# Attention's value products with the values stationary on two column tiles, and ended groups' transposed sums turned back

## What is computed

```
s = jnp.einsum('bqkgd,bnkd->bkgqn', qc, k_cmp)
s = s.astype(jnp.float32) - slopes[:, :, None, None] * dist
p_cmp = masked_softmax(s, dist >= 0)
o_cmp = jnp.einsum('bkgqn,bnkd->bqkgd', p_cmp.astype(dt), v_cmp)
imp = jnp.einsum('bkgqn,nj->bkqj', p_cmp, ov)
...
o = gc[..., 0:1] * o_cmp + gc[..., 1:2] * o_slc + gc[..., 2:3] * o_win
```

## Time and profile before

| | us |
|---|---|
| median of 3 runs | 1056.08 |
| lowest and highest | 1053.9, 1059.67 |
| the profiled execution | 1058.48 |
| its span in the trace | 1056.7 |
| of it, attention (first scores to first SSD transposition) | 273.66 |

### The profile page before, as it was taken

One profiled execution on the slowest core, in us unless ns is written; L12 is line 12 of the kernel. 1 busy time (PEld: TensorE's weight loads), 2 busy tenths in 40 slices (PEclk: granted clock), 3 DMA queues, 4 the chain that ended last, 5 costly groups with the idle time before them and its releaser, 6 DMA issues.

```text
span 1056.7 us, 14288 instructions
## 1 busy us (share of the span) xinstructions
PE 1027.7 (97%) x4759; PEld 617.8 (58%) x4760; DVE 643.5 (61%) x1630; ACT 323.4 (31%) x766; POOL 175.4 (17%) x214
## 2 busy tenths in 40 slices
PE   8999999999999999999999999999989999999997
PEld 4544475444546877778779885555564444444443
DVE  3331121455454777776643898765578688877985
ACT  3321121111133766565665763332110000000000
POOL 0030051111000400000000400211021333323333
PEclk8999999999999999999999999999999999999999
DMA  7310042012000200000000504232649869999432
GB/s 262 103 45 28 1 82 79 1 40 84 20 1 1 81 2 1 1 2 2 1 1 1 200 2 133 100 120 80 238 161 367 294 234 345 338 383 340 137 113 91
DMA packets 73687, 119.23 MB, mean 113 GB/s; under 512 B 14016, under 2 KB 53152, under 8 KB 73632
## 3 DMA queue, kind: packets, MB, share of 16 engines
q1 hardware_dynamic: 62544, 87.55, 24.6%
q0 software_dynamic: 11088, 30.95, 8.3%
HBM read 105.37 MB, written 21.50 MB: 120 GB/s over the span
## 4 chain that ended last, share of the span: by engine, by line
PE 51%; DVE 12%; issue 3%; DMA 3%; ACT 2%; POOL 0%; POOLq 0%; DVEq 0%; ACTq 0%
PE ps L1804 14%; PE ps L1150 9%; PE ps L1814 7%; PE ps L2127 5%; PE ps L1118 4%; PE ps L1129 4%; PE ps L1171 3%; PE ps L2137 2%; DMA big_w<-hn_dram,misc 2%; DVE ring_gate_up L1276 1%; DVE big_w L1618 1%; PE ps L2158 1%; DVE big_u L2346 1%; ACT big_u L1226 1%; DVE misc L291 1%
## 5 line engine op out<-in xcount | busy, mean ns | idle before, releaser
L1618 DVE STREAM_TRANSPOSE big_w<-big_w 32x256 f32<-32x256 f32 x384 | 167.3, 436 | 34.7 <-DMA big_w<-hn_dram,misc 28.4
L1804 PE MATMUL ps<-ring_gate_up,big_w 128*128 (+1 forms) x400 | 179.9, 593 | 1.9 <-DVE big_w L1618 1.5
L517 PE MATMUL ps<-big_w,big_u 128*128 128x512 f32 (+1 forms) x448 | 175.8, 547 | 1.7 <-DMA big_w<-in_w_in 1.7
L517 PEld LDWEIGHTS ps<-big_w,big_u 128*128 128x128 f32 x448 | 84.2, 193 | 78.5 <-issue 71.9
L1804 PEld LDWEIGHTS ps<-ring_gate_up,big_w 128*128 128x128 f32 x400 | 73.9, 190 | 85.6 <-issue 85.6
L1150 PEld LDWEIGHTS ps<-ring_down,big_u 128*128 128x128 f32 x912 | 109.7, 192 | 15.7 <-issue 12.1
L1150 PE MATMUL ps<-ring_down,big_u 128*128 128x65 f32 x912 | 116.3, 273 | 0.5 <-DVE big_w L1303 0.4
L1226 ACT ACTIVATE big_u<-ps 128x512 f32<-128x512 f32 (+1 forms) x126 | 69.4, 582 | 112.9 <-PE ps L1129 112.7
L1276 DVE CUSTOM_DVE_ANT_0 ring_gate_up<-ps,ring_down 128x384 f32<-128x384 f32 (+7 forms) x128 | 73.8, 629 | 43.2 <-PE ps L1118 42.7
L1218 ACT ACTIVATE ring_gate_up<-ring_gate_up,big_w 128x64 f32<-128x64 f32 (+8 forms) x192 | 92.2, 555 | 1.1 <-DVE big_w L1276 1.1
L1814 PE MATMUL ps<-ring_down,big_w 128*128 x200 | 90.0, 593 | 0.6 <-ACT big_w L1848 0.6
(11 more groups left out here) (389 smaller groups left out, 1351.2 us busy)
## 6 DMA issues: line engine op xcount, KB each, us to landing
ring_gate_up<-in_w_gate SPq DMA_DIRECT2D x16, 1024.0 KB, 10.4
ring_gate_up<-in_w_up SPq DMA_DIRECT2D x16, 1024.0 KB, 13.2
ring_down<-in_w_down SPq DMA_DIRECT2D x16, 1024.0 KB, 14.8
misc<-in_x SPq DMA_DIRECT2D x16, 512.0 KB, 4.0
big_w<-in_w_in SPq DMA_DIRECT2D x6, 1024.0 KB, 7.2
big_w<-in_w_out SPq DMA_DIRECT2D x8, 512.0 KB, 5.2
hn_dram<-big_u SPq DMA_DIRECT2D x8, 512.0 KB, 2.6
out<-ring_gate_up SPq DMA_DIRECT2D x8, 512.0 KB, 3.8
```

The lines of the kernel that those rows point to most:

```text
L517: last = nc.tensor.matmul(ps[:, b, 0:width], uT[:, k, c * P:(c + 1) * P], wbuf[:, n % 2, k, 0:width], start=(k == 0), stop=(k == KD - 1))
L1618: last = nc.vector.transpose(dst[j * 32:(j + 1) * 32, :, i * 32:(i + 1) * 32], src[i * 32:(i + 1) * 32, :, j * 32:(j + 1) * 32])
L1804: last = nc.tensor.matmul(ps[:, 2 + b, :], xT[:, b, k, :], ring_gu[:, bass.ds(at + k * 2 * D_EXP, BANK)], start=(k == 0), stop=(k == KD - 1))
```

## The change

In WIN and SEL groups the two operands of the value product change places: 64 columns of values of group g are stationary, on column tile g of the array (output partitions 64g to 64g+63), and the transposed weights of all heads of the slot stream past them, 128, 256 or 512 columns. The blocks are transposed in another order for that (key block, group, head). The sums come out transposed, head dimension by query, in bank 6. When a group has ended, ACT copies them to SBUF (`copy_values`), PE turns them back with four transpositions (`turn_values`), and DVE reads the turned bank. CMP groups keep the weights stationary, now with both groups in one 128-row product against block-diagonal values (L1175 of the new kernel); their product with the overlap table is one of its own (L1170), into another bank, for chunks 4 to 7. The rows' sums of weights no longer come from a column of ones but from the exponentials themselves (`accum_out`). Banks 4, 5 and 7 serve transposed weights, turned sums, importance, selection and the SSD constants in turn. `values(j-2)` runs as a whole ahead of `transposes(j-1)`. WIN and SEL groups are read by DVE one iteration later.

```diff
-        return [(g, r, b) for i, g, r in heads_of(j) for b in range(len(key_blocks(br, c)))]
+        return [(g, r, b) for b in range(len(key_blocks(br, c))) for g in range(NG) for r in pairs]
...
+    turned = [gi for gi, (br, c) in enumerate(groups) if br != CMP]
+    turns_before = lambda gi: sum(1 for x in turned if x < gi)
+    turn_at = {last_slot[groups[gi]] + 3: gi for gi in turned}
+    imp_at = {last_slot[CMP, c] + 2: c for c in sel_count}
+    bank_users, copy_use, sel_use, imp_use, turn_use, prep_use = [], [], {}, {}, {}, None
+    for j in range(J + 3):
+        if j in imp_at:
+            imp_use[imp_at[j]] = len(bank_users)
+            bank_users.append((imp_read, sel_count[imp_at[j]]))
+        if j in turn_at:
...
+            turn_use[turn_at[j]] = len(bank_users)
+            bank_users.append((o_read, turn_at[j] + 1))
...
-            if use >= 2:
-                pe.wait_ge(*bank_users[use - 2])
-            return 4 + use % 2
+            if use >= 3:
+                pe.wait_ge(*bank_users[use - 3])
+            return bank_of(use)
...
-        def values(j, a, b):
+        def bank_is_free(gi):
+
+            if groups[gi - 1][0] == CMP:
+                pe.wait_ge(o_read, gi)
+            else:
+                pe.wait_ge(oT_copied, turns_before(gi))
+
+        def compressed_values(j):
 
             gi, br, c, pairs = slots[j]
-            if a == 0:
-                if j == first_slot[br, c] and gi >= 1:
-                    pe.wait_ge(o_read, gi)
-                pe.wait_ge(wT_done, copies_before[j + 1])
-            blocks = blocks_of(j)
-            w = HD + 17 if br == CMP else HD + 1
-            for x in range(a, b):
-                g, r, blk = blocks[x]
-                if br == CMP:
-                    for g in range(NG):
-                        rows = slice(g * 64, (g + 1) * 64)
-                        last = nc.tensor.matmul(ps[:, 6 + g, r * w:(r + 1) * w], weightsT(j, 0)[rows, x * P:(x + 1) * P],
-                                                v_cmp[rows, 0:w], start=True, stop=True)
-                    continue
-                at = key_blocks(br, c)
-                last = nc.tensor.matmul(ps[:, 6 + g, r * w:(r + 1) * w], weightsT(j, x // 4)[:, (x % 4) * P:(x % 4 + 1) * P],
-                                        vals[br][:, at[blk], g, :], start=(blk == 0), stop=(blk == len(at) - 1))
-            if b == len(blocks) and b > a:
-                last.then_inc(pv_done, 1)
+            pe.wait_ge(wT_done, copies_before[j + 1])
+            rows = [weightsT(j, 0)[:, r * P:(r + 1) * P] for r in pairs]
+            if c in sel_count:
+                bank = transpose_bank(imp_use[c])
+                for r in pairs:
+                    nc.tensor.matmul(ps[:, bank, r * NG * N_BLK:(r + 1) * NG * N_BLK], rows[r], v_cmp[:, NG * HD:CMP_V],
+                                     start=True, stop=True)
+            if gi >= 1:
+                bank_is_free(gi)
+            for r in pairs:
+                last = nc.tensor.matmul(ps[:, O_BANK, r * P:(r + 1) * P], rows[r], v_cmp[:, 0:NG * HD], start=True, stop=True)
+            last.then_inc(pv_done, 1)
+
+        def values(j):
+
+            gi, br, c, pairs = slots[j]
+            if j == first_slot[br, c]:
+                bank_is_free(gi)
+            pe.wait_ge(wT_done, copies_before[j + 1])
+            blocks, m = key_blocks(br, c), len(pairs)
+            for b, blk in enumerate(blocks):
+                for g in range(NG):
+                    x = (b * NG + g) * m
+                    last = nc.tensor.matmul(ps[g * HD:(g + 1) * HD, O_BANK, pairs[0] * P:(pairs[-1] + 1) * P],
+                                            vals[br][:, blk, g, 0:HD], weightsT(j, x // 4)[:, x % 4 * P:(x % 4 + m) * P],
+                                            start=(b == 0), stop=(b == len(blocks) - 1))
+            last.then_inc(pv_done, 1)
+
+        def turn_values(gi):
+
+            pe.wait_ge(oT_copied, turns_before(gi) + 1)
+            bank = transpose_bank(turn_use[gi])
+            for r in range(GQ):
+                last = nc.tensor.transpose(ps[:, bank, r * P:(r + 1) * P], o_T[:, turns_before(gi) % 2, r * P:(r + 1) * P],
+                                           ident[:, :])
+            last.then_inc(o_turned, 1)
...
+            if 2 <= j < J + 2 and slots[j - 2][1] != CMP:
+                values(j - 2)
+            if j in turn_at:
+                turn_values(turn_at[j])
...
-                    z_pieces(piece_at[j][1], piece_at[j][2])
                 transposes(j - 1, k)
-            if n_t == 0 and j in piece_at:
-                z_pieces(piece_at[j][1], piece_at[j][2])
-            if v < n_v:
-                values(j - 2, v, n_v)
...
-                last = nc.scalar.activation(w, w, ACT.Exp, bias=neg[:, br, h:h + 1], scale=-1.0)
+                last = nc.scalar.activation(w, w, ACT.Exp, bias=neg[:, br, h:h + 1], scale=-1.0,
+                                            accum_out=den[c % 2][:, br, h:h + 1])
...
+        def copy_values(gi):
+            act.wait_ge(pv_done, last_slot[groups[gi]] + 1)
+            nc.scalar.activation(o_T[:, turns_before(gi) % 2, :], ps[:, O_BANK, :], ACT.Copy).then_inc(oT_copied, 1)
...
         for j in range(J + 1):
+            if j in turn_at:
+                copy_values(turn_at[j])
...
+            bank = O_BANK if br == CMP else bank_of(turn_use[gi])
+            O = ps[:, bank, :].rearrange("p (r g d) -> p g r d", r=GQ, g=NG)
...
+            dve.wait_ge(exp_done, last_slot[br, c] + 1)
             if br == CMP:
...
+            if br == CMP:
+                dve.wait_ge(pv_done, last_slot[br, c] + 1)
+                o.done(nc.vector.tensor_tensor(dst, O, fb, ALU.mult))
+                dve.sem_inc(o_read, 1)
+                if c in sel_count:
...
+                    dve.sem_inc(imp_read, 1)
...
+                dve.wait_ge(o_turned, turns_before(gi) + 1)
+                nc.vector.tensor_tensor(tmp, O, fb, ALU.mult).then_inc(o_read, 1)
                 dve.wait_ge(o_read, gi + 1)
                 o.done(nc.vector.tensor_tensor(o_att[:, c, :], o_att[:, c, :], M["o_tmp"], ALU.add))
...
+            read_at.setdefault(last_slot[br, c] + (2 if br == CMP else 3), []).append(gi)
...
+        last_values()
```

98 lines of the change are left out of this document (48 added, 50 removed).

## The result

The changed kernel takes 1081.76 us (median of 4 runs, 1079.72 to 1084.93), the kernel before 1055.17 in the same comparison. The ratio is 1.0247 with a 95% interval of 1.0207 to 1.0287: slower by 26.6 us. The profiled execution took 1081.66 us. The forecast was 1076, with a range of 1056 to 1110. The size came out well because two errors of about 15 us each cancelled each other, as the rest of this document shows.

A forecast was written before the change was run, and what follows sets the result against it. PE was taken to bound attention, busy 265.25 of 273.66 us. Work -33, bank 6 waits +35, importance bank +12, other waits +6 gave +20: 1078.5 us on the profiled execution, 1076 against the median, range 1056 to 1110.

The forecast's parts named there:

- PE's own work, -33: PE's work in attention: 50 us of value passes leave; turning back 7.0, importance product 3.5, shape changes 6 come.
- side by side: WIN and SEL value products on two column tiles overlap, 0.11 us per pair of passes, so 50 of 100 us leave.
- The 15 waits for bank 6, 35 us: PE waits for ACT's copy of an ended group's sums before the next group's values: 15 waits, together 35 us.
- four last 2.9 us: On ACT, four exponentials of 384 columns with row sums at 0.22 us each last 2.9 us instead of 2.12.
- The importance bank, 4 x 2.9 = 12: In chunks 4 to 7, the slot's second transposition bank waits for DVE's importance reading: four waits of 2.9 us, 12.
- Waits for weights and the old waits, +6: PE waits for weights to transpose in a dozen more slots, +12; most waits of before go, -6; net +6 us.
- The end of the stage, 0 (-1 to +2): At attention's end, halved last values against the wait for ACT's copy, turning and later SSD work: 0 us in sum.
- The clock, 0 in the sum, 3 to 6 us in the range: Half-clock stretches at new PE waits, up to 1.7 us each: none in the sum, 3 to 6 us in the range.
- the 0.95 that the prediction named as its limit: Sign for the attention stage: the prediction is wrong on the mechanism if the granted clock falls under 0.95.
- one after the other: Rival: value passes on the two column tiles don't overlap, PE has 50 us more; 1112 us, chance 0.15.
- The accumulator costs nothing: Rival: exponentials with row sums keep their pace of 0.505, so no change, 1057 us; chance 0.10.
- The waits are covered: Rival: the copy of sums is done before PE asks, so the kernel gets faster, put at 1040 us; chance 0.11.

The follow-up runs named there:

- no sums: The changed kernel with exponentials that write no row sums, the sums set to one once: 1069.94 us.
- importance late: The changed kernel with only the importance product of a compressed slot put behind the next slot's transpositions, ScalarE's copy staying late: 1070.05 us.
- copy early: The changed kernel with ScalarE's copy of an ended group's sums one slot earlier, ahead of the next weight copies and exponentials: 1050.02 us.
- both moves: The changed kernel with the copy of ended sums one slot earlier and the importance product behind the next slot's transpositions: 1031.47 us, 1031.52 when timed again.
- both, no sums: The kernel with both moves, its exponentials writing no row sums (set to one once): 1028.79 us.
- before with sums: The kernel before, with every exponential writing row sums into columns that nobody reads: 1057.53 us.
- the run on one tile: The kernel with both moves, with both groups' value products on one column tile and no accumulation over key blocks: 1072.38 us.
- The run with the fillings: The changed kernel with 12 useless identity transpositions on TensorE ahead of each of the 15 waits for ScalarE's copy: 1074.70 us.

## Why the prediction was right, and where it was wrong

All kernels in one table. Length, busy and idle time of PE and clock are from the windows of the stage; the difference is to the 273.66 us of before. "Addition" is the slot by slot one with the measured 0.095 us for a row sum, given for the four kernels that the last expectation names; its working isn't printed here, so this column can't be checked from the rows; "clock" is (1 - granted clock) x length, what a busy PE loses at the lower level.

| kernel | length | PE busy | PE idle | clock | addition | + clock | measured |
|---|---|---|---|---|---|---|---|
| changed | 295.6 | 248.7 | 46.9 | 0.95 | +5.5 | +20 | +21.9 |
| no sums | 280.7 | 242.0 | 38.7 | 0.97 | | | +7.0 |
| importance late | 283.5 | 244.4 | 39.1 | 0.96 | -3.2 | +8 | +9.8 |
| copy early | 266.0 | 241.6 | 24.4 | 0.97 | -18.6 | -11 | -7.7 |
| both moves | 247.9 | 235.7 | 12.2 | 0.99 | -29.3 | -27 | -25.8 |
| both, no sums | 243.6 | 232.8 | 10.8 | 1.00 | | | -30.1 |
| before with sums | 277.0 | 267.1 | 9.8 | 0.99 | | | +3.3 |

The 0.095 and the clocks were put in after the runs, except for the kernel with only the importance late, whose time was told first; so the table describes, and 1 to 3 us stay unexplained in each of its four rows. Each row is of one traced execution: that of "no sums" is the fastest of its four, 6 us below their median, and that of "before with sums" the slowest of its eight, 4 us above theirs. The rows of the three kernels whose stage isn't shown above:

```profile
298.44:579.14 280.70, 241.97 (x1853) 159.84 (x1854) 175.29 (x645) 162.66 (x340) 11.86 (x5) 0.97 0.02 9
```

```profile
299.64:543.23 243.59, 232.80 (x1852) 155.35 (x1853) 175.70 (x645) 163.67 (x340) 11.85 (x5) 1.00 0.03 10
```

```profile
301.44:578.42 276.98, 267.14 (x2080) 210.26 (x2081) 175.85 (x645) 177.63 (x519) 11.85 (x5) 0.99 0.03 9
```

Point by point against the prediction's steps:

- **PE's own work, -33: right.** Of the 248.7 us of busy time 15.4 are put down to low clock; the rest is 32 less than the 265.25 of before. With both moves, where one stretch of low clock costs 1.7 us, PE is busy for 235.7, which makes 31. The choice it rests on, side by side, is shown by the run on one tile. Not each term held as well: from the first turning transposition to the next product's start it is 0.44 to 0.75 us in the kernel with both moves (391.08 to 391.83 in the rows above), 9.2 us in the 16 groups, against 16 x 0.44 = 7.0. Which other term made up for the 2 us wasn't separated.
- **The 15 waits for bank 6, 35 us: right in kind and number, 9 us too large.** There are 8 + 7 of them, 0.55 us (CMP 5, below) to 3.14 (SEL 2), 26.2 in all, and they go when the copy moves. The size failed through one term, the row sum of 0.22 in "four last 2.9 us". They last 2.4; with 0.095 the sum of the 15 would have been 35 - (7 x 4 + 8 + 3 x 4 + 4 x 2) x 0.125 = 28. By kind it would have been 16.3 for SEL, where 16.1 were measured (L1188), and 11.1 for CMP, where 10.1 were (L1175).

```profile
456.62 1.16 PE L1175 MATMUL ps<-big_w,big_u 128*128 128x128 f32 x8 [0.55 <-ACT misc L1263]
```

- **The importance bank, 4 x 2.9 = 12: right.** Four waits, 12.7 us, three of 3.0 and one of 3.6. They go when the product moves.
- **Waits for weights and the old waits, +6: wrong, about 0.** All other idle time of PE is 46.9 - 26.2 - 12.7 = 8.0 us, and was 8.4. The wait for exponentials rose from 1.6 to 4.4 us and not by 12. The 0.22 accounts for some 4 of the 9 that are missing (the prediction's rival without a price for the sums took 7 off there, and 0.125 of the 0.22 was too much); the rest is open.
- **The end of the stage, 0 (-1 to +2): its upper end.** 2.0 us are lost behind the stage. The steps were those of the prediction: PE waits 0.70 us for the copy, and then 2.06 for DVE in the SSD's second chunk.
- **The clock, 0 in the sum, 3 to 6 us in the range: wrong, about 15.** The granted clock shows as the 0.95 that the prediction named as its limit; unrounded (15.4 of 295.6 us) it is 0.948, just under it, so by its own sign the prediction was wrong on this part of the mechanism. The step that failed is "I have none in the sum": the earlier trace rows showed a stretch at half clock behind one busy only in part, the sum held 19 waits of 1.6 to 3.8 us, and the prediction let them pass since work lay between. The run with the fillings shows that they bring it, and the kernel with both moves that it leaves with them.

Of the other signs that the prediction named, two on ACT were missed, mostly through the 0.22: ACT is busy for 180 us in the stage and not 210, and the pace of its exponentials at 384 columns is 0.60 and not 0.72.

So waits came out at 38.5 us net instead of 53 (35 + 12 + 6), the clock at 15 instead of 0, and the work at -32. The sum of +20 met +21.9 because the two misses cancel.

Of the rivals, "one after the other" (1112) is refuted by two runs. "The accumulator costs nothing" was nearer to the truth than my 0.22, and yet its time of 1057 was not: the changed kernel without any sums takes 1070, since most of the waits for the copy stay (20.8 us of 26.2 in its trace) and part of the low clock with them. "The waits are covered" names the gain that was to be had, 1030 to 1040: with the copy done before PE asks, and the importance out of the way, the kernel takes 1031.5 us.

The scatter agrees with a price of the clock of its own. The four runs of the changed kernel without sums, one program, by mean granted clock over the whole span:

| granted clock | 0.988 | 0.983 | 0.982 | 0.977 |
|---|---|---|---|---|
| us | 1063.94 | 1069.22 | 1070.66 | 1076.68 |

0.011 of clock go with 12.7 us, and 0.011 x 1064 is 11.7. The runs of this kernel lie 1.2% apart; nine runs of the kernel with both moves, which waits neither for the copy before its values nor for the importance bank, lie within 0.4% (1030.57 to 1034.56).

The change itself is good. It leaves 30 us of work out, and loses them by where two steps stand: a copy behind exponentials that it doesn't need, and a product whose bank is read late, ahead of transpositions that need the bank.

## What to carry to other kernels

When a change gives an engine's single output buffer a new reader, place that reader in its own engine's order by when its data is complete, ahead of anything that waits for work behind it: here one slot earlier was worth 32 us, more than the change's whole effect. Price TensorE's new waits in two parts where the granted clock stands at 1.00 before: as idle time, and for the work behind them at half clock (26 and 13 us of waits came with 15 us of clock). Before a row of another stage decides between two readings, look at all in which it differs from the new case; the row on the same tiles had a stride, and the squares had a semaphore wait behind each that the exponentials don't have.

## What the runs showed of the hardware that I had not expected

- Useless work in waits of TensorE made the kernel 7.1 us faster: 180 transpositions in waits of the same length, with the granted clock in the stage at 0.98 instead of 0.95.
- A row sum on ACT costs 0.095 us per exponential at 384 columns (pace 0.60 instead of 0.505) and as much at 512 (0.705 instead of 0.61), though its reading instruction shows as 0.20 us, and a square of 512 columns with an accumulator showed 0.22 from the reading instruction to the next square.
- Two fp32 products on two column tiles run side by side: 656 passes in 58.3 us against 107.1 on one tile. The Trainium skill ("TensorEngine Tiling (Array Packing)", Key Properties) has tiles load and multiply in parallel, and its Performance Considerations name this swap; the runs agree with both. Of what the swap brings with it, a copy and a turning back for each group, the waits were the larger part: 26 us of waiting for the copy against 9 us of turning.
- A streamed fp32 operand with a stride of 16 elements doubled the time of 64 products, from 3.68 to 7.13 us.
